# One attention layer: both key tiles projected first, rotation by lane shuffle, heads paired on row and column halves, mask and maximum in one step, the sink as a column

## The reference, cut to what matters

```
ql, kl rotated: x*cos + rotate_half(x)*sin
logits = q . k / 8;  masked outside the window
m = max(max(logits), sink)
p = exp(logits - m);  denom = sum(p) + exp(sink - m)
o = (p / denom) . v
```

## Time and profile before

| what | value |
|---|---|
| median of three executions | 2054.65 us (2053.88 to 2057.94) |
| profiled execution, its own time | 2064.9 us |
| its span, first to last instruction | 2063.1 us |
| busy PE, DVE, ACT, POOL | 1968.5, 1188.6, 692.5, 22.4 us |
| mean granted TensorE clock | 0.971 |
| chain of work that ended last | PE 89%, DVE 7%, ACT 2% |

### The profile page before, as it was taken

How to read it: one execution, slowest core, us unless ns; L and a number is a source line. 1 busy time by engine, 2 the same in 40 slices (tenths; PEclk the granted TensorE clock), 3 DMA queues, 4 the chain that set the end, 5 groups by cost and what they waited for, 6 DMA issues and landing times.

```text
span 2063.1 us, 26084 instructions
## 1 busy us (share of the span) xinstructions
PE 1968.5 (95%) x10860; PEld 1648.1 (80%) x10860; DVE 1188.6 (58%) x2032; ACT 692.5 (34%) x1053; POOL 22.4 (1%) x18
## 2 busy tenths in 40 slices
PE   4999999999888999999999999999899899999997
PEld 2999999999877888888888888775565578888885
DVE  3456566555763566526552565665255369668485
ACT  3333333333322333213321233345235344233242
POOL 0000000000220000000000000000000000000000
PEclk8999999999998999999999999989989999999998
DMA  6221222112201133323322332110010023233333
GB/s 273 92 76 48 82 82 83 47 67 82 82 1 46 36 130 106 102 96 109 123 89 95 123 112 73 65 42 1 21 41 1 31 80 94 93 102 92 95 100 102
DMA packets 45332, 165.82 MB, mean 80 GB/s; under 512 B 4896, under 2 KB 5280, under 8 KB 45088
## 3 DMA queue, kind: packets, MB, share of 16 engines
q1 hardware_dynamic: 45216, 164.16, 23.8%
HBM read 162.05 MB, written 2.10 MB: 80 GB/s over the span
## 4 chain that ended last, share of the span: by engine, by line
PE 89%; DVE 7%; ACT 2%; DMA 1%; issue 1%; SPq 0%; DVEq 0%
PE slot L390 27%; PE slot L379 8%; PE slot L381 8%; PE slot L380 8%; PE MA L541 4%; PE slot L791 4%; PE slot L792 4%; PE slot L793 4%; PE slot L726 3%; PE MB L448 2%; PE MA L791 2%; PE MA L792 2%; PE MA L793 2%; PE slot L717 2%; PE MB L481 1%; DMA AD<-in_ada 1%
## 5 line engine op out<-in xcount | busy, mean ns | idle before, releaser
L1184 DVE TENSOR_TENSOR WL<-WR,WH 128x1024 fp32r<-128x1024 f32 x204 | 249.4, 1224 | 227.3 <-ACT WH L846 226.2
L846 ACT ACTIVATE WH<-WR 128x1024 fp32r<-128x1024 f32 x204 | 215.4, 1057 | 399.3 <-DMA WR<-in_w 399.3
L379 PE MATMUL slot<-HH,WH 128*128 128x384 f32 (+2 forms) x896 | 324.1, 362 | 24.1 <-DVE HL L1280 11.0
L380 PE MATMUL slot<-HL,WH 128*128 128x384 f32 (+2 forms) x896 | 310.6, 347 | 0.0
L381 PE MATMUL slot<-HH,WL 128*128 128x384 f32 (+2 forms) x896 | 310.5, 347 | 0.0
L379 PEld LDWEIGHTS slot<-HH,WH 128*128 128x128 f32 x896 | 171.0, 191 | 55.0 <-issue 28.7
L390 PE MATMUL slot<-HH,WH 128*128 128x256 f32 (+1 forms) x768 | 199.4, 341 | 2.5 <-DVE ACC L1507 1.6
L390 PE MATMUL slot<-HH,WL 128*128 128x256 f32 (+1 forms) x768 | 196.6, 338 | 0.0
L390 PE MATMUL slot<-HL,WH 128*128 128x256 f32 (+1 forms) x768 | 195.8, 337 | 0.0
L380 PEld LDWEIGHTS slot<-HL,WH 128*128 128x128 f32 x896 | 171.3, 191 | 8.9 <-issue 2.2
L381 PEld LDWEIGHTS slot<-HH,WL 128*128 128x128 f32 x896 | 170.7, 191 | 8.5
(11 more groups left out here) (232 smaller groups left out, 3162.1 us busy)
## 6 DMA issues: line engine op xcount, KB each, us to landing
WR<-in_w SPq DMA_DIRECT2D x204, 512.0 KB, 3.6
ada_raw<-in_ada SPq DMA_DIRECT2D x84, 512.0 KB, 4.6
AD<-in_ada SPq DMA_DIRECT2D x3, 2048.0 KB, 23.6
X<-in_x SPq DMA_DIRECT2D x1, 3072.0 KB, 12.2
out<-Y SPq DMA_DIRECT2D x8, 256.0 KB, 2.2
Y<-in_masks SPq DMA_DIRECT2D x1, 512.0 KB, 19.8
ada_raw<-in_rope SPq DMA_DIRECT2D x1, 512.0 KB, 3.8
small<-in_small SPq DMA_DIRECT2D x1, 327.5 KB, 2.9
```

The source lines that it names most:

```text
L379: mm(SLOT[s][:, po], WH[w % NB][:, k, :], hi[:, k, to], start=(k == 0), stop=False)
L380: mm(SLOT[s][:, po], WH[w % NB][:, k, :], lo[:, k, to], start=False, stop=False)
L846: go(WH[t % NB][:, :, :], WR[t % NB][:, :, :], ACT.Copy).then_inc(w_hi_done, 1)
L1184: tt(WL[t % NB][:, :, :], WR[t % NB][:, :, :], WH[t % NB][:, :, :].bitcast(F32), ALU.subtract).then_inc(w_split, 1)
```

## The change

1. Order. Both key tiles are projected first, twelve weight tiles in a row (`at_projections`, with two sets of KH, KO, QH, QO, AV), and then one loop runs over all 64 units (`attention`). The value transposes of the first key tile go to MB between the projections. The buffers PT, PT5 and part of PB now lie where HH and HL lie, the other PB where the `ada_raw` buffers lie.
2. Rotation. L693 and the matrix product go. VectorE permutes RAW within groups of 32 partitions (`stream_shuffle` to ROT), multiplies it with the sine, whose sign is now in the table, and adds. ScalarE rounds the sum to the high part (`rounded`), VectorE forms the low part after it (`rope_low`). In ScalarE's program `rounded` of a tile stands behind the evacuation of the next.
3. Pairs. `UNITS` has the two halves innermost. `at_scores_of(k)` issues each product for part 0 (rows 0 to 63, to MB) and at once for part 1 (rows 64 to 127, to MA). `at_values` issues each value tile for part 0 (columns 0 to 63) and part 1 (columns 64 to 127) next to each other, in pieces of two tiles, over the following pairs.
4. Mask and maximum. The mask products (L709) go. One VectorE instruction (`tensor_tensor_reduce`) adds a bf16 mask `edge` to the scores, scales by -1/8, writes them to PB in SBUF and gives the minimum together with the negative sink: the negative maximum. It takes the place of L1628 and L1636. ScalarE's exponential then works within PB.
5. Sink. GpSimd writes the negative sink of each unit into the column behind its last key tile (`sink_columns`), so the exponential's sum holds it. L1122 and L1632 go.
6. Copies. The transposes of a pair go to two halves of slot 0, four tiles each; the fifth tiles of four units are gathered in slot 1 and copied together.

```diff
-        UNITS = [(bi, half, r) for bi in range(LAT // P) for half in range(2) for r in range(4)]
+        UNITS = [(i, bi, r, half) for i in range(2) for bi in range(LAT // P) for r in range(4) for half in range(2)]
+        LEAD = 2
...
+            def sink_columns():
+                pool.wait_ge(nsink_ready, 1)
+                for u in range(len(UNITS)):
...
+                    if u >= NPB:
+                        pool.wait_ge(p_turned, u - NPB + 1)
+                    pool.tensor_scalar(PB[u % NPB][:, n * P:n * P + 1], nsink[:, hd:hd + 1], 1.0, 0.0, ALU.mult, ALU.add).then_inc(sink_col, 1)
...
+            def at_projections():
+                first_tiles(TOK, LAT)
+                third_tile(LAT)
+                full_tile(1, LAT, HH, HL)
+                full_tile(0, LAT, HH, HL)
+                full_tile(1, TOK, HH, HL)
+                full_tile(0, TOK, HH, HL)
+                pe.wait_ge(evacuated[1], tile.half(1))
+                value_turns(MB)
+                for j in range(4):
+                    full_tile((j + 1) % 2, LAT, HH, HL)
+                full_tile(1, TOK, HH, HL)
...
+            def at_scores_of(k):
+                i, bi, r, _ = UNITS[2 * k]
+                pe.wait_ge(roped, 5 * i + 2 + r)
+                if k >= 1:
+                    pe.wait_ge(row_max, 2 * k)
...
+                for po, to in ((slice(PC0, PL0), slice(0, CTX)), (slice(PL0, PL0 + n * P), lat)):
+                    for e, (a, b) in enumerate(((QH, KH), (QH, KO), (QO, KH))):
+                        for part, S in enumerate((MB, MA)):
+                            hp = slice(64 * part, 64 * part + 64)
+                            last = mm(S[:, po], a[i][hp, r, q], b[i][hp, to], start=(e == 0), stop=(e == 2))
+                last.then_inc(at_scores, 2)
...
+            def at_values(v, cs):
...
+                for c in cs:
+                    for part in range(2):
+                        hp = slice(64 * part, 64 * part + 64)
+                        probs = PT[v % 2][part][:, c, :, :] if c < 4 else PT5[v % 2][:, :, part, :]
+                        last = mm(SLOT[1][hp, 512:1024], AV[i][:, at[c], hp], probs, start=(c == 0), stop=(c == n + 1))
...
+                for k in range(PAIRS):
+                    if k + LEAD < PAIRS:
+                        at_scores_of(k + LEAD)
+                    at_turn(2 * k)
+                    at_turn(2 * k + 1)
+                    if k >= 4:
+                        v, n = k // 4 - 1, chunks(8 * (k // 4 - 1))
+                        cs = ((0, 1), (2, 3), (4,), ())[k % 4][:max(0, n - 2 * (k % 4))]
+                        if cs:
+                            at_values(v, cs)
...
+                for k in range(PAIRS):
+                    at_copy(2 * k)
+                    at_copy(2 * k + 1)
+                    for u in range(2 * k + 2 * LEAD, min(2 * k + 2 * LEAD + 2, len(UNITS))):
+                        at_exp(u)
...
+            def masked_max(u):
...
+                nc.vector.tensor_tensor_reduce(PB[u % NPB][:, 0:n * P], (MB, MA)[part][:, PC0:PC0 + n * P], edges(bi), -AT_SCALE,
+                                               nsink[:, hd:hd + 1], ALU.add, ALU.min, nmax[u % 4][:, :]).then_inc(row_max, 1)
...
+                for k in range(PAIRS):
+                    for u in range(2 * k + 2, min(2 * k + 4, len(UNITS))):
+                        scaled_probs(u)
+                    for u in range(2 * k + 2 * LEAD, min(2 * k + 2 * LEAD + 2, len(UNITS))):
+                        masked_max(u)
```

More of the change, by code:

```diff
@@ L685, in _ @@
             norm_pe(0)
[L686 to L695, removed]
-                hp = slice(64 * half, 64 * half + 64)
-                S = (MB, MA)[u % 2]
-                first, n = window(bi)
-                if u >= 2:
-                    pe.wait_ge(probs_ready, unit.times(1, (u - 1)))
-                q = slice(bi * P, (bi + 1) * P)
-                parts_of = [(QH, KH), (QH, KO), (QO, KH)]
-                for e, (a, b) in enumerate(parts_of):
-                    mm(S[:, PC0:PL0], a[hp, r, q], b[hp, 0:CTX], start=(e == 0), stop=(e == 2))
-                edges = ([(0, 0)] if bi > 0 else []) + ([(n - 1, 1)] if bi < LAT // P - 1 else [])
-                for e, (a, b) in enumerate(parts_of):
-                    mm(S[:, PL0:PL0 + n * P], a[hp, r, q], b[hp, CTX + first * P:CTX + (first + n) * P], start=(e == 0), stop=False)
-                for e, (at, which) in enumerate(edges):
-                    last = mm(S[:, PL0 + at * P:PL0 + (at + 1) * P], tri[:, 2, :], tri[:, which, :], start=False, stop=(e == len(edges) - 1))
-                last.then_inc(at_scores, 1)
@@ L718, in at_turn @@
                 last.then_inc(p_turned, 1)
-            def at_values(v, bi, half):
+            def at_values(v, cs):
+                i, bi, _, _ = UNITS[8 * v]
                 first, n = window(bi)
-                pe.wait_ge(pt_ready, unit.times(1, (4 * v + 4)))
-                if half == 0 and bi > 0:
-                    pe.wait_ge(at_out, block_n.times(1, bi))
-                for j, c in enumerate([0, 1] + [CCH + first + j for j in range(n)]):
-                    last = mm(SLOT[1][64 * half:64 * half + 64, 0:512], AV[:, c, 64 * half:64 * half + 64],
-                              PT[v % 2][:, j, :, :].rearrange("p r q -> p (r q)"), start=(j == 0), stop=(j == n + 1))
-                last.then_inc(pv_done, 1)
@@ new lines, in at_values, with attention @@
+                if cs[-1] == n + 1:
+                    last.then_inc(pv_done, 1)
+            def attention():
+                at_scores_of(0)
+                pe.wait_ge(evacuated[0], tile.half(1))
+                pe.wait_ge(evacuated[1], tile.half())
+                value_turns(SLOT[0])
+                at_scores_of(1)
+                pe.wait_ge(v_ready, vals.now(-2))
+                for k in range(PAIRS):
[8 more added lines that the diff above has]
+                            at_values(v, cs)
+                at_values(BLOCKS - 1, range(chunks(8 * (BLOCKS - 1))))
+                pe.wait_ge(at_out, BLOCKS)
@@ L1656, in two_key_heads @@
-                for u in range(len(UNITS) + 2):
-                    softmax(u, i)
-                    w = u - 4
-                    if w % 8 == 0 and w > 0:
-                        at_evac(w // 8 - 1, i)
-                at_evac(3, i)
-                unit.add(32)
-                pair.add(8)
-                tile.add(6)
+                rope_low(5 * i)
+                for j in range(1, 5):
+                    rope_sums(5 * i + j)
+                    split_low(first + j + 3)
+                    rope_low(5 * i + j)
```

306 lines of the change are left out of this document (164 added, 142 removed).

## The result

The changed kernel takes **1963.95 us** (median of 4 runs, 1961.07 to 1965.7) beside 2056.3 us for the kernel before on the same chip: a ratio of 0.9554, 95% interval 0.9539 to 0.9569, 92 us less. In the profiled executions the span falls from 2063.1 to 1962.6 us, by 100.5; that is more than 92 because the execution of the kernel before that was profiled (2064.9 us) lies 9 us above this median. The forecast was 1977 with a range of 1952 to 2014.

The account below looks back on a forecast made before the run. TensorE was taken as the limit half of the time, three engines taking turns otherwise. Projections 67 plus attention 146 (132 and 14 for the clock) make 213 against 291.4; saving 78 from 2054.65 gives 1977 us, range 1952 to 2014.

Parts of the forecast that it names:

- Projections: Both projection stretches, 83.9 us before: less rotations 9.3, weight-split wait 5.1 and half clock 3.1, small additions; about 67 us.
- seam: Between attention and second projections: TensorE's 5.10 us wait for a weight split goes, with 3.1 us lost at half clock.
- TensorE's pair: Attention, two heads on TensorE: 3.2 us with row and column halves overlapping in full, 5.0 us all serial.
- the column row: Trace evidence for overlap: 16 records on four column quarters take 1.92 us, against 10 in 4.50 without overlap.
- the second rival: Attention on TensorE: the halves do not overlap, 5.0 us a pair, saved 48, total 2007 us; chance 0.13.
- VectorE and ScalarE: Attention, busy time for two heads: VectorE 3.25 us with mask-and-maximum at 0.80, ScalarE 3.0 us.
- T+3.1: Attention: time when ScalarE's two copies end, counted from T, when both maxima of pair k+1 are done.
- The loop: Attention: scores, transposes, copies, exponentials, scaling, maxima take 7.3 us per two pairs, 3.65 each; 132 us with ends and waits.
- one fifth of 70, 14 us: Attention: half clock throughout would make it 200 us, 70 more than full clock; one fifth of that was taken.
- 213: Whole attention layer's stage after the change: 67 us projections plus 146 us attention, where it was 291.4.
- The rival with no clock loss: Attention takes 130 us without low clock, stage 197, saved 94, total 1960 us; chance 0.14.
- The rival that the clock stays low: Attention stays at half clock, 200 us, stage 267, saved 24, total 2030 us; chance 0.12.

Follow-up runs that it names:

- shuffle_alone: Kernel before, with the rotation product replaced by VectorE's lane shuffle, the high part still rounded by VectorE: 2042.84 us, ratio 0.993.
- the ladder: Three runs on the changed kernel, cumulatively adding mask products, the sink's exponential and addition, then the exponential reading scores from PSUM: 1965.94, 1974.29, 2016.31 us.
- scores_held_for_exp: Changed kernel plus mask products, sink as exponential and addition, and the exponential reading PSUM, so the next scores wait for ScalarE: 2016.31 us.
- values_serial: Changed kernel with each piece's value products issued for all of part 0, then all of part 1: 1963.24 us.
- mask_and_exp_apart: Changed kernel with mask by products, plain maximum and a small step, exponential from PSUM, sink as exponential and addition: 2017.94 us.

## Why the prediction was right, and where it was off

*Projections*: 67 predicted, 65.3 measured. The sum of removed rotations, seam and clock holds; the seam was shown by itself (8 us), the rotation is 0.93 us in the trace of shuffle_alone, VectorE's shuffle is 0.733 where 0.693 stood for it, and neither it nor the late low parts hold anything up: TensorE idles for 0.55 us in the whole stretch.

*TensorE's pair*: both halves overlap in full, as taken from the column row. The value products come at 0.43 us per couple of records as forecast. The run with one row half shows what the other end of the bound costs for the products: 22 us, some 17 of them without its low clock, where the second rival (2007 for both kinds) had 0.79 x 32 = 25. For the values no run shows it.

*VectorE and ScalarE*: mask and maximum 0.81 for 0.80; VectorE 96.47 / 32 = 3.0 us a pair for 3.25, ScalarE 2.9 for 3.0. GpSimd's column costs nothing where it stands; the ladder puts the sink's two steps on ScalarE and VectorE at 8 us, 6 of them at full clock. (In the forecast's loop two exponentials of 0.83 from T+3.1 end at T+4.76 and not at T+4.85, and the words before the projections' sum take off less than its last term; both are tenths of a microsecond.)

*The loop*: 30 x 3.65 + 5, start 7, end 9, waits 2 = 132 without the clock. Measured are 112.8 us from the second pair's maximum to the last, and 15.7 around them: 128.5 with the clock, some 125.5 without. Its mechanism, which the forecast worked out from "the products of pair k+2 wait for both maxima of k+1", is what scores_held_for_exp shows: put the exponential in the maximum's place and the pair goes from 4.12 to 5.47 us.

*The term that was mis-sized is the clock*: "one fifth of 70, 14 us". In the middle the fall cost 1.5 us: one distance between maxima is 5.2 us where values_serial, whose clock did not fall there, has 3.7, and the 27 distances at full clock in both runs are equal within 0.01 us. At the start one distance at half clock is 4.5 us (1408.1 to 1412.6) where the next, at full clock, is 3.1. No run with this order of work has full clock there, so the second 1.5 is an estimate; together 3 us. What the forecast had wrong is how long the clock is low. One fifth of its 200 us is 40 us; measured are about 10 (0.96 over 128.5 us). Its price for a microsecond at half clock, 14/40, was near the measured 3/10. The clock did not fall in the second half of each block, where TensorE is busy for 3.6 of 6 us (1432 to 1438, clock 1.00); it fell once more in the middle, in this execution and not in that of values_serial, and what brings that fall no run shows. So about 11 of the 19 us by which the stage came out shorter than 213 are the clock, 6.5 the loop with its ends (132 against 125.5), 1.7 the projections. The median shows only 13 of the 19: the forecast read its saving in an execution of 2064.9 us and took it off a median of 2054.65, and that hid a part of the miss. The rival with no clock loss (1960) described the kernel better than the forecast.

*The rival that the clock stays low* (2030) did not happen, and the reason given against it is borne out for the start: with products on one half only it stayed at 0.50 for 30 us. Later in that run, with value products in between, it stayed at 1.00. What part the transposes have in it no run shows, since all of them have the transposes.

*Not in the forecast*: why the one step on VectorE matters. I priced it as an instruction (0.80 for 0.757 + 0.214). As an instruction it was worth 2 us at most, where the scores are held for ScalarE; that its output in SBUF frees the scores before ScalarE comes is worth 42, of which the loop itself has some 28 and the low clock that comes with the longer loop some 14.

Left open: what the value halves are worth, alone or together with the row halves (the edit meant to take their overlap away did not), what the merged copies (6) bring, and what one attention loop instead of two brings by itself (1). No run undid these.

## What to carry to other kernels

Where three engines pass one buffer round, look for the instruction that frees it and for what is queued ahead of that instruction on its engine; moving the release one engine earlier brought 42 us, fewer steps on VectorE at most 2 in a kernel where VectorE was not what the others waited for. An edit that is meant to undo an overlap must be looked at in the trace first: reordering the products left most of it standing. Put work that is ready ahead of work that waits in an engine's order (8 us), and spread what can be spread over the period (4 us). Price a low clock by how long it will last (10 us of it cost 3), and its cure by the ready work that it stands in front of.

## What the runs showed of the hardware

- TensorE starts a later product on a free row half before earlier ones on the other half: seventh issued at 1448.90, fourth at 1449.01. Issued one half after the other, twelve products take 1.13 us, in alternating order 0.82, all on one half 1.54; eight records on two column halves take 1.94 in either order.
- Two row halves cost the same 0.12 us a couple as one half alone: full overlap, no loss, for 256 columns.
- With products of 64 rows on one half and transposes the granted clock stayed at 0.50 (1.2 GHz) for 30 us with TensorE busy for 29.38; with both halves it was back at 1.00 (2.4 GHz) after some 7 us, and stayed there in 1432 to 1438 with 3.6 busy us in 6. Products on one half with value products in between ran at 1.00 for 112.8 us.
- Mask, scale, sink and maximum over 128x640 in one VectorE instruction take 0.88 us, a plain maximum of that size 0.82 (in mask_and_exp_apart): the second operand and the full output cost 0.06.
